# A weight sum added by GpSimd instead of by an accumulating transfer, and table angles and token sums moved in order, in a two-block transformer kernel

## The reference, cut to what matters

```python
def swiglu(x, w_gate, w_up, w_down):
    return (jax.nn.silu(x @ w_gate) * (x @ w_up)) @ w_down      # 1024 -> 2816 -> 1024
# block 1, twice:  x += 0.5*norm(swiglu(norm(x)));  x += norm(mixer(norm(x)));  x += 0.5*norm(swiglu(norm(x)));  gated embedding
# block 2, twice:  x += mixer(norm(x));             x += swiglu(norm(x))
# the mixers hold attention with rotary tables: cos and sin of position * frequency
```

## Time and profile before

| | us |
|---|---|
| median of 3 runs (3544.0 to 3549.39) | 3545.88 |
| the profiled execution | 3554.07 |
| its span | 3552.9 |
| PE busy | 3308.3 (93%) |
| DVE busy | 2224.6 (63%) |
| POOL busy | 1878.8 (53%) |
| ACT busy | 1218.7 (34%) |
| mean granted TensorE clock | 0.972 of full |

### The profile page before, as it was taken

How to read it: one execution, slowest core, us unless ns; L and a number is a source line. 1 busy time by engine, 2 the same in 40 slices (tenths; PEclk the granted TensorE clock), 3 DMA queues, 4 the chain that set the end, 5 groups by cost and what they waited for, 6 DMA issues and landing times.

```text
span 3552.9 us, 51458 instructions
## 1 busy us (share of the span) xinstructions
PE 3308.3 (93%) x19276; PEld 2777.1 (78%) x19281; DVE 2224.6 (63%) x2541; ACT 1218.7 (34%) x2167; POOL 1878.8 (53%) x899
## 2 busy tenths in 40 slices
PE   7899999989979899999989997998999999999998
PEld 6898775788867798877568986766689988878986
DVE  5669444576875766835366685669566753466681
ACT  4441215344313444122534431423434411144430
POOL 5339762532667334975162376655253497733365
PEclk9999999999989999999999998999999999999999
DMA  4553230256422365322035642221146533215643
GB/s 150 152 153 114 89 89 30 83 145 164 128 89 96 108 166 143 103 89 85 23 95 149 165 121 90 77 89 54 36 131 166 148 100 109 83 58 144 172 118 95
DMA packets 107754, 390.90 MB, mean 110 GB/s; under 512 B 11952, under 2 KB 12208, under 8 KB 107312
## 3 DMA queue, kind: packets, MB, share of 16 engines
q1 hardware_dynamic: 88704, 320.90, 28.0%
q0 software_dynamic: 15552, 56.63, 9.8%
q10 hardware_dynamic: 3312, 10.87, 0.8%
HBM read 384.16 MB, written 4.19 MB: 109 GB/s over the span
## 4 chain that ended last, share of the span: by engine, by line
PE 48%; DVE 15%; DMA 15%; issue 9%; POOL 7%; ACT 5%; POOLq 0%; DVEq 0%; SPq 0%; ACTq 0%
DMA raw<-in_ws 14%; PE psC L730 3%; PE psC L731 3%; PE psC L732 3%; POOL raw L646 3%; PE psA L730 3%; PE psA L732 3%; PE psA L731 3%; DVE WL L1949 2%; PE psC L825 2%; POOL WH L609 2%; PE psC L827 2%; PE psC L826 2%; POOL WL L611 2%; DVE HIDL L2003 2%
## 5 line engine op out<-in xcount | busy, mean ns | idle before, releaser
L609 POOL TENSOR_TENSOR WH<-raw,scalars 128x1024 fp32r<-128x1024 f32 (+1 forms) x338 | 663.7, 1964 | 814.0 <-DMA raw<-in_w 745.7
L611 POOL TENSOR_TENSOR WL<-raw,WH 128x1024 fp32r<-128x1024 f32 (+1 forms) x338 | 822.4, 2433 | 26.5
L1949 DVE TENSOR_TENSOR WL<-raw,WH 128x1024 fp32r<-128x1024 f32 x378 | 498.9, 1323 | 315.4 <-POOL raw L646 202.1
L1516 ACT ACTIVATE WH<-raw 128x1024 fp32r<-128x1024 f32 x378 | 396.8, 1053 | 143.2 <-DMA raw<-in_ws 143.2
L635 POOL DMA_DIRECT2D raw<-in_ws x108 | 93.9, 870 | 444.3 <-DMA raw<-in_ws 433.8
L2003 DVE TENSOR_TENSOR HIDL<-HID,HIDH 128x512 fp32r<-128x512 f32 x132 | 308.0, 2396 | 0.0
L646 POOL TENSOR_TENSOR raw<-raw,raw 128x1024 f32<-128x1024 f32 x54 | 129.2, 2393 | 316.7 <-DMA raw<-in_ws 311.1
L730 PE MATMUL psA<-HH,WH 128*128 128x512 f32 x560 | 234.3, 418 | 33.8 <-DVE Y L1940 33.8
L730 PE MATMUL psC<-HIDH,WH 128*128 128x512 f32 x528 | 210.8, 399 | 40.5 <-ACT Y L1609 40.5
L731 PE MATMUL psA<-HH,WL 128*128 128x512 f32 x560 | 221.6, 396 | 0.0
L732 PE MATMUL psA<-HL,WH 128*128 128x512 f32 x560 | 221.5, 396 | 0.0
(11 more groups left out here) (475 smaller groups left out, 9312.1 us busy)
## 6 DMA issues: line engine op xcount, KB each, us to landing
raw<-in_w SPq DMA_DIRECT2D x338, 512.0 KB, 3.6
raw<-in_ws SPq DMA_DIRECT2D x270, 512.0 KB, 4.5
raw<-in_ws POOLq DMA_DIRECT2D x108, 512.0 KB, 5.7
X<-in_x ACTq DMA_DIRECT2D x4, 512.0 KB, 9.6
NRAW<-in_mem ACTq DMA_DIRECT2D x2, 1024.0 KB, 6.5
out<-Y SPq DMA_DIRECT2D x8, 256.0 KB, 2.2
POSI<-in_pos ACTq DMA_DIRECT2D x4, 256.0 KB, 4.3
PRAW<-in_p ACTq DMA_DIRECT2D x2, 512.0 KB, 5.1
```

What stands on the lines that cost most here:

```text
L609: pool.tensor_tensor(WH[j][:, 0:w], raw[j][:, 0:w], zero[:, 0:1].broadcast_to([P, w]), ALU.subtract).then_inc(w_hi, 1)
L611: pool.tensor_tensor(WL[j][:, 0:w], raw[j][:, 0:w], WH[j][:, 0:w], ALU.subtract).then_inc(w_split, 1)
L1516: act.activation(WH[slots[i]][:], raw[slots[i]][:], ACT.Copy).then_inc(part_hi, 1)
L1949: dve.tensor_tensor(WL[slots[i]][:], raw[slots[i]][:], WH[slots[i]][:], ALU.subtract).then_inc(part_lo, 1)
```

## The change

**The sum c+d.** d has a buffer of its own in raw form, `DX`, 4 KB that held `US`; `hidden` puts the up half into HID instead. SyncE loads d into `DX`, GpSimd adds `DX` to c. So d is read from HBM once in a pair, and one of the two accumulating DMAs is gone. The wait on SyncE ahead of d is for `part_lo` of operand 6, and d is ahead of c in the queue. High and low part of operand 6 are made first in a pair (after operand 2's low part) instead of last.

**The order.** `hidden(0)` and the first silu stand ahead of BF and the token sums, the second silu behind TH. The table angles are computed in one go ahead of the sums of squares, their sines ahead of the first output chunk.

```diff
-    GS, US = Y[:, 0:2], Y[:, 2:4]
+    GS = Y[:, 0:2]
+    DX = Y[:, 2:4].rearrange("p a n -> p (a n)")
@@ SyncE, ffn, the loop over pairs
                 part(slots[0], v, 0, a_in)            # now part(a, ...)
+                sp.wait_ge(part_lo, n.full(part_lo, 4))
+                n.full(part_lo, PRODUCTS - 4)
+                part(DX, v, 2, d_in)
                 sp.wait_ge(part_used, n.full(part_used))
-                part(slots[1], v, 1, c_in)
+                part(c, v, 1, c_in)
...
-                sp.wait_ge(part_used, n.full(part_used, 2))
-                part(slots[6], v, 2, d_in)
+                n.full(part_used, 2)
@@ GpSimd, sums
             pool.wait_ge(c_in, n.full(c_in, 16))
-            add_to(slots[1], v, 2, cd_in)
+            pool.wait_ge(d_in, n.full(d_in, 16))
+            pool.tensor_tensor(raw[slots[1]][:], raw[slots[1]][:], DX, ALU.add).then_inc(sum_ready, 1)
+            pool.wait_ge(sum_ready, n.full(sum_ready))
...
-            pool.wait_ge(cd_in, n.full(cd_in, 16))
@@ TensorE, product
-            pe.wait_ge(part_lo, n.full(part_lo))
+            if i != 6:
+                pe.wait_ge(part_lo, n.full(part_lo, 2 if i == 3 else 1))
@@ ScalarE, pair and ahead of it
+                high(6)
                 high(3)
...
-                high(6)
...
+            silu(0)
             for k in range(KD):
                 act.activation(BF[:, k], X[:, k], ACT.Copy, scale=gain(k)).then_inc(bf_ready, 1)
-            silu(0)
-            silu(1)
             for i in (0, 2, 1, 3):
                 act.wait_ge(tf_ready, n.full(tf_ready))
                 act.activation(TH[i][:], TF[i][:], ACT.Copy).then_inc(th_ready, 1)
+            silu(1)
@@ ScalarE, behind the down projection: all sines (and the two table stores) ahead of outputs()
@@ VectorE, hidden
-                dve.tensor_tensor(US[:, j], up_bank(m), RS[:], ALU.mult).then_inc(gu_free, 1)
+                dve.tensor_tensor(HID[:, m], up_bank(m), RS[:], ALU.mult).then_inc(gu_free, 1)
...
-                dve.tensor_tensor(HID[:, m], US[:, j], GS[:, j], ALU.mult)
+                dve.tensor_tensor(HID[:, m], HID[:, m], GS[:, j], ALU.mult)
@@ VectorE, pair and ahead of it
                 low(2)
+                low(6)
...
-                low(6)
...
+            hidden(0)
             dve.wait_ge(bf_ready, n.full(bf_ready, KD))
             ... the four token sums ...
-            hidden(0)
             hidden(1)
@@ VectorE, behind the down projection
-                outputs(((1, newF), (2, newI)) if embedding else ((0, tabM),))
+                for inv, tab in ((1, newF), (2, newI)) if embedding else ((0, tabM),):
+                    angle(inv, tab, 0)
+                    angle(inv, tab, 1)
+                outputs()
```

More of the change, by code:

```diff
@@ L530, in border, with part @@
             ring(RING, RING + 2)
-        def part(slot, v, j, s):
-            sp.dma_start(raw[slot][:], A["ws"][bass.ds((v - 1) * 4 + j, 1)].rearrange("a p n -> p (a n)")).then_inc(s, 16)
+        def part(to, v, j, s):
+            sp.dma_start(to, A["ws"][bass.ds((v - 1) * 4 + j, 1)].rearrange("a p n -> p (a n)")).then_inc(s, 16)
         def ffn(normed=True):
@@ L550, in ffn @@
             plain = n.now(piece_used) - UP_PIECES
+            a, c, b, a2 = (raw[slots[i]][:] for i in (0, 1, 3, 4))
             v = n.room(pair_index)
             sp.wait_ge(piece_used, plain + used[0])
-            part(slots[0], v, 0, a_in)
+            part(a, v, 0, a_in)
             sp.wait_ge(piece_used, plain + used[1])
-            part(slots[1], v, 1, c_in)
-            part(slots[4], v, 0, a2_in)
+            part(c, v, 1, c_in)
             sp.wait_ge(piece_used, plain + used[2])
-            part(slots[6], v, 2, d_in)
+            part(DX, v, 2, d_in)
+            part(a2, v, 0, a2_in)
             sp.wait_ge(piece_used, plain + used[3])
-            part(slots[3], v, 3, b_in)
+            part(b, v, 3, b_in)
             with n.loop(PAIRS - 1):
@@ L563, in ffn @@
                 sp.wait_ge(part_used, n.full(part_used))
-                part(slots[0], v, 0, a_in)
+                part(a, v, 0, a_in)
+                sp.wait_ge(part_lo, n.full(part_lo, 4))
+                n.full(part_lo, PRODUCTS - 4)
+                part(DX, v, 2, d_in)
                 sp.wait_ge(part_used, n.full(part_used))
-                part(slots[1], v, 1, c_in)
+                part(c, v, 1, c_in)
                 sp.wait_ge(part_used, n.full(part_used, 2))
-                part(slots[3], v, 3, b_in)
+                part(b, v, 3, b_in)
                 sp.wait_ge(part_used, n.full(part_used))
-                part(slots[4], v, 0, a2_in)
-                sp.wait_ge(part_used, n.full(part_used, 2))
-                part(slots[6], v, 2, d_in)
+                part(a2, v, 0, a2_in)
+                n.full(part_used, 2)
+            n.full(part_lo, PRODUCTS)
             sp.wait_ge(part_used, n.full(part_used, 4))
@@ L1510, in high @@
             def high(i):
-                landing = (a_in, cd_in, None, b_in, ac_in, None, d_in)[i]
+                landing = (a_in, None, None, b_in, ac_in, None, d_in)[i]
                 if landing is None:
@@ L1515, in high @@
                     act.wait_ge(landing, n.full(landing, 16))
[L1516 removed]
+                act.activation(WH[slots[i]][:], DX if i == 6 else raw[slots[i]][:], ACT.Copy).then_inc(part_hi, 1)
             def quad_gate(i, bank):
@@ L1586, in ffn @@
                 return
-            outputs(3, (tabM,) if layer is None else (newF, newI), down_bank)
+            tabs = (tabM,) if layer is None else (newF, newI)
+            tables_for(ACT.Sin)
+            for i in range(2 * len(tabs)):
+                tab = tabs[i // 2][:, i % 2]
+                act.wait_ge(tab_arg, n.full(tab_arg))
+                act.activation(tab, tab, ACT.Sin).then_inc(tab_ok, 1)
+                n.full(tab_ok)
+            tables_for(LOG_EXP)
+            if len(tabs) > 1:
+                act.wait_ge(tab_ok, n.now(tab_ok))
+                for k, tab in zip("FI", tabs):
+                    load(saved[k], tab[:], tab_saved)
+            outputs(3, down_bank)
         def squares_room(m):
@@ L1594, in squares_room, with outputs @@
                 n.full(yss_step)
-        def outputs(pieces, tabs=(), early_bank=None):
-            if tabs:
-                tables_for(ACT.Sin)
+        def outputs(pieces, early_bank=None):
             for m in range(KD):
@@ L1609, in outputs @@
                 act.activation(Y[:, m], bank, ACT.Copy).then_inc(out_free, 1)
-                if m < 2 * len(tabs):
-                    tab = tabs[m // 2][:, m % 2]
-                    act.wait_ge(tab_arg, n.full(tab_arg))
-                    act.activation(tab, tab, ACT.Sin).then_inc(tab_ok, 1)
-                    n.full(tab_ok)
-                    if m == 2 * len(tabs) - 1:
-                        tables_for(LOG_EXP)
-                        if len(tabs) > 1:
-                            act.wait_ge(tab_ok, n.now(tab_ok))
-                            for k, tab in zip("FI", tabs):
-                                load(saved[k], tab[:], tab_saved)
         def to_tokens(which):
@@ L1947, in low @@
                 if i in (0, 2):
-                    dve.wait_ge(sum_ready, n.full(sum_ready))
-                dve.tensor_tensor(WL[slots[i]][:], raw[slots[i]][:], WH[slots[i]][:], ALU.subtract).then_inc(part_lo, 1)
+                    dve.wait_ge(sum_ready, n.full(sum_ready, 2 if i == 0 else 1))
+                dve.tensor_tensor(WL[slots[i]][:], DX if i == 6 else raw[slots[i]][:], WH[slots[i]][:], ALU.subtract).then_inc(part_lo, 1)
             def scale(bank, half, sign):
```

8 lines of the change are left out of this document (2 added, 6 removed).

## The result

The changed kernel takes 3448.22 us (median of 4 runs, 3447.4 to 3453.28), the kernel before it 3544.94 us on the same chip (4 runs, 3543.4 to 3549.39): a ratio of 0.9728, with a 95% interval of 0.9711 to 0.9745. The forecast was 3450 us. A later comparison of the same kernel gave 3450.42 us (5 runs) and a ratio of 0.9709 (0.9686 to 0.9732).

What follows compares the result with a forecast made beforehand. TensorE, busy 93%, was taken as the base load, stalled by waits on pair-weight DMAs. 3554.07 - 105.2 + 9 + 0 = 3457.9, the profiled execution being 8.19 above the median, so 3450 us; range 3410 to 3515.

Steps and rivals of the forecast that it cites:

- pairs: Six pair stages, 54 pairs: from 22.4 us each to 20.10 with TensorE the bound, 105.2 us gained after allowances.
- ahead of the pairs: Before each stage's pair 0: gate 3's stall moves there, starting it 1.5 us later, +9 us, bounds -18 and +24.
- chunks behind angles: Behind the down projection: angles in one go, chunks 0 to 3 copied after the last sine; 0, bounds 3 either way, twice.
- bound of 113: Pair stages: upper bound of the gain, 123 - 10 us, with no wait left.
- slack of 3.75 us: In each pair, from slot 1's freeing to product 0: new chain 10.6 us against 14.35 for the five products between.
- early enough: SyncE's new wait: operand 6's low part comes 3.6 or 4.8 us into the pair, slot 1 is free at 5.7.
- sign I had set: Forecast is wrong if SyncE's wait for operand 6's low part ends after slot 1 is free.
- three mishaps together: Pair chain: d ahead of c 1.5 us, additions 3.23 each, low part 1.74; 14.3 in all, still not above 14.35.
- rival of 8.7: SyncE's two loads follow each other in full, c takes 8.7 us, pairs 21.8 in the middle: 3524 us, chance 0.11.
- if nothing collides: Ahead of the pairs, second stage: pair 0 starts at 731.37 - 3 = 728.4, 3 us earlier.
- rival in which everything is excluded at every pair: VectorE and GpSimd exclude each other in everything, 23.6 us a pair: slower, 3620 us, chance 0.05.
- the stall of gate 3 goes for good: Ahead of the pairs: VectorE's chain is shorter than thought, saving 40 us and the 9 of delay: 3401 us, chance 0.06.

Runs made afterwards that it cites:

- e2_moves_only: Kernel before the change with only the moves (hidden(0), first silu, angles in one go), d still added by accumulating DMA: 3543.06 us, ratio 1.0006.
- e4_add_twice: Changed kernel with the addition that makes operand 2 done twice in every pair, same result: 3548.98 us, ratio 1.0031 to the kernel before.
- e10_twice_c_first: e4_add_twice with SyncE issuing c before it waits for operand 6's low part and issues d: 3538.97 us, ratio 0.9983 to the kernel before.
- e1_sum_only: Changed kernel with hidden(0), the two first silu and the angles put back where they were: 3447.58 us, ratio 0.9745 to the kernel before.
- e7_chunks_first: Changed kernel copying output chunks 0 to 4 before the first sine, chunk 5 before the third, sums of squares between angles: 3411.86 us, ratio 0.9605.
- e14_twice_early_seed: e4_add_twice with operand 6's parts earlier, gate 3's silu behind the seed copy, weighing behind operand 3's low part: 3489.57 us, ratio 0.9843.
- e8_both: e7_chunks_first plus the third addition of a stage's first pair waiting for the TL subtractions: 3407.9 us, ratio 0.9596 to the kernel before.
- e11_twice_plain: e4_add_twice with the remaining accumulating DMA made plain, so operand 4 lacks a summand: 3509.96 us, ratio 0.99 to the kernel before.

## Why the prediction was right, and where not

The sum, in spans of the profiled executions: 3552.9 before, 3447.2 after, 105.7 less. The terms:

```
                       forecast    measured
pairs                   -105.2      -115.2
ahead of the pairs        +9         +10.1
chunks behind angles       0          +1.8
not assigned                          -2.4
sum                      -96.2      -105.7
```

By the medians the kernel became 96.7 us shorter (3544.94 to 3448.22), by the profiled executions 105.7, because that of the kernel before took 8.19 us more than its median and that of the changed kernel only 0.24. So the 10 us that the pairs gained beyond the forecast and the 8.19 taken off at its end nearly cancel in 3450, which is closer to the measured time than the pairs' term is to its own. Whether the 8.19 lay in the pairs is not shown. `e2_moves_only` speaks for it: its pairs are those of before, and in an execution of 3538.24 us their stages sum to 1195.3, 13 less than the 1208.4 of the execution of 3554.07.

- **The pairs: mechanism right, size 10 us short.** The accumulating DMA of d left the chain and TensorE became the bound. I had taken 20.10 a pair and 8.1 us for single pairs that still wait. The pairs take 20.0 (54 x 0.1 = 5.4 us), and the two that wait cost 1.6 instead of 8.1. Against that the cold start of a stage cost 1.5 to 2.6 us, 12.0 in all, where 1.6 each and 9.7 were forecast. The result is nearer the bound of 113 than the value taken.
- **The slack of 3.75 us: wrong.** This is the step that failed, though it did not move the time. It followed one chain, from the freeing of slot 1 to product 0. `e4_add_twice` showed 22.1 us a pair for 2.6 us more, where this chain alone, 10.6 + 2.6 = 13.2 against 14.35, would still fit. The tightest way goes round through VectorE: the low part of operand 0, in its order the low part of operand 6, then d. Its 21.6 less 2.6 leave 0.9 us of room, and 0.5 on average. I had priced the new wait of SyncE as "early enough" with the low part of operand 6 ending 3.6 to 4.8 us into the pair. In an ordinary pair it does (4.5, and slot 1 is free 1.4 later); that holds only while the low part of operand 0 is early. By the sign I had set (that wait ending after slot 1 is free) it does happen, in two pairs of the second stage, where TensorE waits 1.1 us in all and the pairs are 1.6 us longer. So the three mishaps together (3.7 us more) would not have been free, as the forecast said: the loop has room for a quarter of them at most.
- **How c lands: mostly as forecast.** From its issue to the first addition 3.7 to 6.9 us pass, 4.5 at the median; the forecast had 4.36, or 5.9 with d in front of it, and the slowest pair lies above that. The rival of 8.7 did not come. `e10_twice_c_first` shows that d ahead of c in the queue costs little.
- **Ahead of the pairs: right in kind and size.** The stall moved from gate 3 to product 0, and three additions took their price from VectorE: from the start of gate 2's piece to product 0 it is +2.7, +1.1, -0.2, +0.8, +2.9 and +2.8 us in the six stages, against 1.5 each. `e1_sum_only` adds what the forecast had left joint: this price comes with the addition, not with the move, for the stall in front of gate 3 grows from 8.4 to 12.6 in the old order. I had given the moved order part of the blame; by `e2_moves_only` (1.0006) it has none that can be measured. The third stage lost nothing because the kernel before was late there already, 36.7 us for this way against 33.4 to 33.9 in the other three stages of block 1; why it was wasn't tried. Two bounds of this part rest on less than they seem to: the 3 us earlier of "if nothing collides" come with no working, and the 0.9 "paid already" is the gap between the low part and pair 0, while the row itself had 2.7 paid (5.18 for 2.48).
- **Exclusion of the engines: as the forecast took it, where they meet.** A GpSimd addition of 128x1024 beside a VectorE operation with two SBUF inputs cost VectorE, as the rows above show, 6.66 for 2.48 and 13.40 for 4.62. The Trainium skill (SBUF — State Buffer, section "SBUF: two separate sides") has the later of the two wait for the whole of the earlier. The trace agrees: in the fifth stage every subtraction ends 1.1 us after an instruction of GpSimd and every addition 2.2 to 2.3 after a subtraction, so each waits for the whole of the other, in turns of 3.3 us. The rival in which everything is excluded at every pair did not come: pairs take 20.0 with GpSimd busy for 7.7 us of each.
- **Chunks: forecast 0, measured +1.8.** `e7_chunks_first` shows what the angles' order could have given: 38.6 us. Computing them in one go leaves chunk 4's copy behind the last sine, 21.1 us late. The changed kernel moves the angles but not that copy. In one go they also gained less than the 7 us forecast. In the first of these stages the four angles end 53.5 us after the start of the first, against 57.2 before with the sums of squares between. As the forecast feared, they fall among GpSimd's splits: the first three take 15.0 to 17.0 us each, the fourth, with GpSimd idle, 5.0.
- **Rival "the stall of gate 3 goes for good" (3401 us):** ruled out by `e2_moves_only` and by the trace after.
- **The range.** The bounds of the terms add up to 3409 and 3506, which is near the stated 3410 to 3515. The "own range" of 3425 to 3485 comes with no working.

Left open: what the 2.4 us not assigned are, why single loads of c take up to 6.9 us, and whether the order of `e14_twice_early_seed` would gain anything on top of `e8_both`; none was tried.

## What to carry to other kernels

When a long step leaves a chain, the room that is left is not that of this chain but of the tightest loop through the engines' program orders; an added dummy instruction of known length measures it in one run (its length less what the round grew by: here 2.6 less 2.05), and the longer wait shows where the next limit stands. Each reordering that freed one loop here exposed the next (22.1, 21.6, 20.8 us a pair on average), so count the round trips of every engine that two steps share before calling a slack. A move of work within an engine's order gained nothing measurable here while the last instruction that TensorE needs stayed where it was: `hidden(0)` moved, and TensorE waited for the TL and the first low part instead; the angles moved, and the copy of chunk 4 stayed behind them. In `e7_chunks_first` that copy moved, and gave 39 us.

## What the runs showed of the hardware

An accumulating DMA takes twice the transfer engines' time of a plain one for the same bytes. In a window of the changed kernel (134 to 154 us; packets, MB, share of 16 engines), as in the earlier trace rows:

```profile
q1 hardware_dynamic: 720, 2.62, 40.6%
q0 software_dynamic: 144, 0.52, 15.5%
```

That is 15.5% of the window a MB for the plain ones (q1) and 29.8% for the accumulating one (q0). That it is the adding and not the queue, `e11_twice_plain` shows: the same bytes on the same queue took 2.6% of the 16 engines over its run (second row), where the accumulating ones of `e4_add_twice` took 4.8% (first row).

```profile
q0 software_dynamic: 7776, 28.32, 4.8%
q0 software_dynamic: 7776, 28.32, 2.6%
```

With the plain write the first addition came 0.9 us sooner after d's issue (medians), and the issue took GpSimd 0.57 us instead of 0.87. So the accumulating DMA that the change removes probably relieved the loads that stay as well; that was not separated from the rest of its gain.
